# Gate and output products of a hybrid attention layer: one product of 512 moving columns, or two of 256

## The reference, cut to what matters

```python
h = jnp.einsum('bsd,de->bse', x, w_in[l]) + b_in[l]
qa, ka, va, qb, kb, vb, qc, z = jnp.split(h, split_idx, axis=-1)
oa, _ = banded_causal_attention(...)      # window 128, 8 heads, sinks
ob = dilated_attention(...)               # three dilations, 4 heads
oc = memory_attention(...)                # 256 memory tokens, 4 heads
y = jnp.concatenate([rms_normalize(oa...), rms_normalize(ob...), rms_normalize(oc...)], axis=-1)
y = y * g_branch[l].astype(jnp.float32) * jax.nn.silu(z.astype(jnp.float32))
y = jnp.einsum('bse,ed->bsd', y.astype(x.dtype), w_out[l])
x = layer_norm(DEEPNORM_ALPHA * x + y, ln_gain[l], ln_bias[l]).astype(x.dtype)
```

## Time and profile before

| | |
|---|---|
| median of 3 runs | 513.6 us |
| the profiled execution: time / span | 513.56 us / 511.6 us |
| TensorE, MATMUL busy | 489.7 us (96%) |
| TensorE, weight load busy | 446.4 us (87%) |
| VectorE busy | 328.3 us (64%) |
| ScalarE busy | 214.9 us (42%) |
| GpSimd busy | 72.7 us (14%) |
| granted TensorE clock, mean | 0.995 |

### The profile page before, as it was taken

The page is one execution under the profiler, slowest core; times in us unless marked ns, Lnnn a source line. Parts: engine busy times, 40 slices in busy tenths (PEclk is TensorE's granted clock), DMA queues, the critical chain, the costliest instruction groups (busy, mean ns, idle before and its releaser), DMA issues.

```text
span 511.6 us, 9694 instructions
## 1 busy us (share of the span) xinstructions
PE 489.7 (96%) x3480; PEld 446.4 (87%) x3480; DVE 328.3 (64%) x908; ACT 214.9 (42%) x488; POOL 72.7 (14%) x53
## 2 busy tenths in 40 slices
PE   4999999999999999999999898999989999999993
PEld 4999999999999988888888787898878788888882
DVE  4776645457565753444444568878897969798734
ACT  5532122002201235555463659655444454444530
POOL 0000000000000000111101101023222323231425
PEclk9999999999999999999999999999999999999998
DMA  8965372638632344532323179424232424241022
GB/s 289 377 209 139 108 222 82 206 115 258 207 124 83 103 133 135 157 90 58 103 84 92 53 234 316 100 63 137 70 127 59 151 53 148 62 143 47 1 83 82
DMA packets 51711, 67.83 MB, mean 133 GB/s; under 512 B 9553, under 2 KB 41297, under 8 KB 51665
## 3 DMA queue, kind: packets, MB, share of 16 engines
q1 hardware_dynamic: 51088, 66.17, 41.2%
q10 hardware_dynamic: 576, 1.05, 0.6%
HBM read 51.18 MB, written 16.02 MB: 131 GB/s over the span
## 4 chain that ended last, share of the span: by engine, by line
PE 81%; DVE 8%; SPq 3%; ACT 2%; DMA 2%; issue 1%; POOLq 0%; POOL 0%; ACTq 0%; DVEq 0%
PE long_ps L951 15%; PE o_ps L910 9%; PE wide L773 8%; PE wide L775 8%; PE wide L774 8%; PE long_ps L850 5%; PE long_ps L852 5%; PE long_ps L851 5%; PE narrow L890 4%; PE wide L878 4%; PE wide L879 3%; DMA mem_raw<-in_mem_t 2%; SPq L575 2%; PE narrow L928 1%; SPq L579 1%
## 5 line engine op out<-in xcount | busy, mean ns | idle before, releaser
L773 PE MATMUL wide<-x_hi,w_hi 128*128 128x256 f32 x320 | 89.8, 280 | 0.3 <-DVE w_lo L1181 0.3
L774 PE MATMUL wide<-x_lo,w_hi 128*128 128x256 f32 x320 | 89.3, 279 | 0.0
L775 PE MATMUL wide<-x_hi,w_lo 128*128 128x256 f32 x320 | 89.3, 279 | 0.0
L773 PEld LDWEIGHTS wide<-x_hi,w_hi 128*128 128x128 f32 x320 | 60.1, 188 | 0.5 <-issue 0.4
L775 PEld LDWEIGHTS wide<-x_hi,w_lo 128*128 128x128 f32 x320 | 60.2, 188 | 0.0
L774 PEld LDWEIGHTS wide<-x_lo,w_hi 128*128 128x128 f32 x320 | 59.8, 187 | 0.0
L1032 ACT ACTIVATE spill<-turn 128x512 fp32r<-128x512 f32 x21 | 13.3, 632 | 103.3 <-DVE turn L1263 76.6
L951 PE MATMUL long_ps<-wo_hi,y_hi 128*128 128x512 f32 x128 | 53.1, 414 | 0.0
L1512 POOL TENSOR_TENSOR g_lo<-g_raw,g_hi 128x1024 fp32r<-128x1024 f32 x6 | 14.3, 2386 | 272.5 <-ACT g_hi L1037 272.5
L951 PE MATMUL long_ps<-wo_lo,y_hi 128*128 128x512 f32 x128 | 52.3, 409 | 0.0
L951 PE MATMUL long_ps<-wo_hi,y_lo 128*128 128x512 f32 x128 | 51.8, 404 | 0.0
(11 more groups left out here) (154 smaller groups left out, 1206.7 us busy)
## 6 DMA issues: line engine op xcount, KB each, us to landing
q_spill<-spill SPq DMA_DIRECT2D x32, 256.0 KB, 2.5
q_pair<-q_spill SPq DMA_DIRECT2D x128, 64.0 KB, 2.0
w_raw<-in_w_qkv SPq DMA_DIRECT2D x12, 512.0 KB, 5.1
x_raw<-in_x_t SPq DMA_DIRECT2D x16, 256.0 KB, 7.8
g_raw<-in_w_gate SPq DMA_DIRECT2D x8, 512.0 KB, 3.8
q_pair<-q_spill SPq DMA_DIRECT2D x32, 128.0 KB, 2.7
q_pair<-q_spill SPq DMA_DIRECT2D x128, 32.0 KB, 1.8
wo_raw<-in_w_out SPq DMA_DIRECT2D x8, 512.0 KB, 4.7
```

The source lines that it names most:

```text
L773: pe.matmul(dst, w_hi[s][:, k, f], t_hi[:, k, cols], start=(k == 0), stop=False)
L774: pe.matmul(dst, w_hi[s][:, k, f], t_lo[:, k, cols], start=False, stop=False)
L775: mm = pe.matmul(dst, w_lo[s][:, k, f], t_hi[:, k, cols], start=False, stop=(k == KT - 1))
```

## The change

A gate or output product over 512 moving columns becomes two products over 256 (`C` is 256, `HALF` is 512), with the same stationary operand, into the left and the right half of the same PSUM bank. The first product into a bank alone carries the start flag.

```diff
-                cols = slice(h * HALF, (h + 1) * HALF)
-                dst = long_ps[n % 2][:, :]
+                dst = long_ps[n % 2]
                 for k in range(share * KT // shares, (share + 1) * KT // shares):
-                    pe.matmul(dst, g_hi[f % 2][:, k, :], x_hi[:, k, cols], start=(k == 0), stop=False)
-                    pe.matmul(dst, g_hi[f % 2][:, k, :], x_lo[:, k, cols], start=False, stop=False)
-                    mm = pe.matmul(dst, g_lo[f % 2][:, k, :], x_hi[:, k, cols], start=False, stop=(k == KT - 1))
+                    for g, x_part in ((g_hi, x_hi), (g_hi, x_lo), (g_lo, x_hi)):
+                        for lo in range(0, HALF, C):
+                            first = k == 0 and g is g_hi and x_part is x_hi and lo == 0
+                            mm = pe.matmul(dst[:, lo:lo + C], g[f % 2][:, k, :],
+                                           x_part[:, k, h * HALF + lo:h * HALF + lo + C], start=first,
+                                           stop=(k == KT - 1 and g is g_lo), skip_group_check=True)
                 if share == shares - 1:
                     mm.then_inc(gate_full, 1)
...
-                    mm = pe.matmul(long_ps[half][:, :], y, w[:, k, half * HALF:(half + 1) * HALF],
-                                   start=(k == 0 and p == 0), stop=(n == half_done[half]))
+                    for lo in range(0, HALF, C):
+                        mm = pe.matmul(long_ps[half][:, lo:lo + C], y, w[:, k, half * HALF + lo:half * HALF + lo + C],
+                                       start=(k == 0 and p == 0 and lo == 0), stop=(n == half_done[half]),
+                                       skip_group_check=True)
                     if n == half_done[half]:
                         mm.then_inc(out_full, 1)
```

## The result

The changed kernel took 516.3 us (median of 12 runs, 515.63 to 518.71), the kernel before 514.5 us (median of 12, 513.48 to 515.84). The ratio is 1.0067 with a 95% interval of 1.0038 to 1.0096: slower, by 0.4 to 1.0%, or 2 to 5 us. The two medians by themselves lie only 1.8 us apart. Forecast were 517.0 us and, over the 513.6 us of the first three runs, +3.5 us. The profiled execution has a span of 514.6 us against 511.6 us, so +3.0 us. These are single executions: the one of before lies 0.9 us under its median, the one of the changed kernel 0.2 us over it.

What follows compares the result with a forecast made beforehand. TensorE's own pace was taken to bound the kernel. Gate +2.1, output +1.55 and end -0.1 us made +3.5 us on 513.56, stated as 517.0 us, range 513.2 to 519.4 us.

Steps and rivals of the forecast that it cites:

- TensorE's own pace sets the time: Gate and output stages: TensorE, busy 96% of the span and almost never idle there, decides the time.
- 720 loads more, none dropped: Gate and output products: 720 become 1440, each with its own weight load, so 720 loads more.
- Pitch of a half: Gate and output halves of 256 columns: starts 117.7 ns apart, taken from projections with `x` moving; swapped roles gave 113.2.
- The second load is hidden: Gate and output halves: a load's pace of 105 ns fits below 117.7 ns, so the added load costs nothing more.
- Change of kind: First long product behind short ones: some 90 ns extra, paid once a run before and after, costed at nothing.
- the rival that doubled it: Both halves of each run's first long product pay the 90 ns: 9 us more, about 526 us; chance 0.03.
- The sum: Whole kernel: gate +2.1, output +1.55 and end -0.1 us, together +3.5 us.
- Gate: 336 gate products: 6.4 ns more each, 2.15 us, of which 97% on the path: +2.1 us.
- Output: 384 output products: 4.6 ns more each, 1.77 us, of which 88% on the path: +1.55 us.
- the chain's share: Output stage: the chain of waits holds 76.5 of 87.2 us of output products, so 88% of the cost counts.
- The end: Last output product, before the last residual sum: takes 0.28 us instead of 0.39, so -0.1 us.
- The rule of fixed cost: Gate and output splits: N/2.4 + 2.5 ns a product makes 1.8 us for 720, ending at 515.4 us; not followed.

Runs made afterwards that it cites:

- the table: Stretches of six profiles: kernel before, changed kernel, only gate or only output products halved, halves reordered, projections widened in pairs with four banks; spans 508.8 to 514.6 us.
- the uneven cut: Against the kernel before, each of the 720 gate and output products cut into 384 and 128 columns instead of 256 and 256: 548.81 us, ratio 1.068.
- four pieces: Against the kernel before, each of the 720 gate and output products cut into four of 128 columns: 662.4 and 672.7 us.
- paired projections: Against the kernel before, 960 projection products of 256 columns became 480 of 512, pairs of jobs sharing two of three wide banks: 521.99 us, ratio 1.0174.
- output halves alone: Against the kernel before, only the 384 output products halved, gate products left at 512 columns: 515.3 us, ratio 1.0034.

## Why the prediction was right, point by point

- **TensorE's own pace sets the time.** Right. Every kernel of the table moved by what its products changed in pitch, apart from the lower clock and from waits in front of the first output product, which vary by some tenths of a microsecond.
- **720 loads more, none dropped.** Right: 4200 and 4200.
- **Pitch of a half.** The choice of 117.7 ns was right (117.5 and 118), and half of the reason given for it holds: products of 256 columns with `x` moving go at 117 to 118 ns in all eight profiles that have them. The other half was wrong. I held that 113.2 belonged to the other place of the operands. The changed kernel's own L784 to L786, untouched by the change and 113.2 ns apart in the earlier trace rows, go at 118 ns in its profile:

```profile
31.41 0.28 PE L784 MATMUL wide<-w_hi,x_hi 128*128 128x256 f32 x1
...
32.83 0.28 PE L784 MATMUL wide<-w_hi,x_hi 128*128 128x256 f32 x1
```

  12 pitches in 1.42 us are 118.3 ns. The same instructions on the same addresses take the one pace or the other in different executions. They do so within one execution too: in the kernel before L784 to L786 go at 113.3 ns until 36 us and at 118.2 ns from 40 to 44 us. So the earlier trace rows showed no price of a place. For the output halves, with `wo` moving, 117.7 ns came true, but no run shows that the place of `wo` is the reason; that may be luck.
- **The second load is hidden.** Right for 256 columns, but by a hair. I took the pace of a load as 105 ns, from 0.84 us for a run of eight. In such runs the first pitch is recorded as 57 ns and the others as 110 to 112; the floor is 112 ns, and 256 columns at 117.5 lie 5 ns above it.
- **Change of kind.** The 90 ns of the earlier trace rows are no price. Before, the second long product starts 0.05 + 0.32 us behind the last transpose; after the change the third half does so with the same two distances:

```profile
212.85 0.29 PE L892 MATMUL narrow<-ident,prob 128*128 128x128 f32 x1
212.90 0.48 PE L852 MATMUL long_ps<-x_hi,g_hi 128*128 128x256 f32 x2
213.22 0.40 PE L852 MATMUL long_ps<-x_lo,g_hi 128*128 128x256 f32 x2
```

  Over the 26 places of this kind the medians from the last transpose to the second long product are 0.344 us before and 0.348 us after, and that is 0.109 for the transpose and 0.235 to 0.239 for the 512 columns. So the start of a product behind a short one seems to be recorded early; the uneven cut shows the same, 384 columns 0.06 us behind a piece of 128. Costing it at nothing was right, and the rival that doubled it had nothing to stand on.
- **The sum.** The terms were right in kind and too large in size, in both stages. Gate: +2.1 us forecast, +2.0 measured, but of these only 1.6 are the products. In their 28 runs, from the first start to that of the next other product, the sum rose from 79.39 to 81.14 us, so by 1.75 us: 5.2 ns a product and not 6.4, and 1.6 us of it came through. The whole product was read from 7 pitches of 228.6 ns, while over the stage it takes about 230. That 2.0 came out so near is therefore in part luck with the waits behind. Output: +1.55 forecast, +1.2 measured. In all 73 runs of output products (the last one to its end) the sum rose from 97.15 to 98.81 us, so by 1.66 us where the pitches gave 1.77. Of this 1.2 us, 73%, came through where the chain's share gave 88%; the other 0.5 us went into TensorE's idle time, which fell from 3.1 to 2.6 us. The end, -0.1, was a slip: the last half starts one pitch behind its other half, so the pair ends 0.39 us behind its start (506.14 above) just as the whole product did, and the term is nothing. Shown for the products are 1.6 + 1.2 = 2.8 us, against the forecast's 3.5.
- **The rule of fixed cost.** By the rule N/2.4 + 2.5 ns, which the Trainium skill (TensorE: Matmul & The Clock Gate, Back-to-back issue gap) gives for isolated products, a split would cost 2.5 ns. The measured cost is 5 to 6 ns in the gate stretch (235 against 229 to 230). The uneven cut, which by that rule should cost the same 2.5 ns, costs 60 (290 against 229 to 230).

Still open: what puts products of 256 columns at 113 or at 118 ns, whether a load of fewer than 128 columns would lower the floor in these products, and whether the few executions at 508 to 511 us of several of these kernels are those in which more products go at the faster pace. No profile caught one of them.

## What to carry to other kernels

When TensorE sets the time, count products as well as columns, and read their price from the distance of two starts. A product with a weight load of 128 columns did not go below a floor here (112 ns, nearly what 256 columns take), and above it each product still costs some ns: make the moving operand as wide as the bank allows, and look for stages where halves can be joined rather than split. Joining them only pays if results are read in time, so give a coarser step the banks it needs, and don't let the last step before a new stage grow.

## What the runs showed of the hardware

- One product of float32r (the kernel's type for these operands, four bytes) with its load of 128 columns takes 109 to 112 ns at least, however few columns move: 112 ns for 128 columns (four pieces), 110 to 112 for 66 columns (value products), 109 for a transpose of 128. 256 columns take 113 to 118 ns, 512 columns 226 to 232, on average 229 to 231 ns, all at the full clock.
- A tile that is already in the array is loaded again at full price: 4200 loads for 4200 products in the changed kernel, and 117.5 ns a half with many repeated tiles against 117.1 ns with fewer.
- The clock was at its lower level behind a wait of TensorE of 4.07 us in the paired projections, and behind one of 1.64 us (output halves alone) and one of 1.63 us (four pieces) at the same place in front of the first output product. It held behind 1.12 and 1.25 us there, but also behind 1.93 us in another stage, so the length of the wait alone does not decide it. The fall cost 1.65 us with the output halves alone (clock 0.89 over 15 us) and 10 us with four pieces (0.50 over 20 us).
